# Softmax scaling moved to ScalarE, and weight splits and the filter network moved in the engines' orders, in a two-block fp32 network

## The chip, the cores and the metric

One core of a Trainium2 chip runs the whole program. Five engines work beside each other and meet at semaphores: PE (TensorE) multiplies matrices, DVE (VectorE) and ACT (ScalarE) do elementwise work and read PSUM, POOL (GpSimd) does elementwise work in SBUF, SP (SyncE) issues most DMA transfers. Each engine takes its own instructions in the order in which they are written. The metric is the device time of one execution in microseconds (us).

## The reference

All is fp32, on 256 tokens of 1024 features. A first block gets modulation vectors from `c` (adaLN), mixes tokens by a Hyena convolution and by neighbourhood attention (NA) over 8 heads, and ends in a mixture of experts by product keys (PEER). A second block has two layers of attention, a state-space scan and a gated network. Cut to what the change touches:

```python
def adaln(cond, p):                       # c and c_ctx
    m = jax.nn.silu(cond) @ p['w_ada'] + p['b_ada']
...
def hyena_filters(L, p):
    h = jnp.sin(freq * (feats @ p['hy_f1_w'] + p['hy_f1_b']))
    h = jnp.sin(freq * (h @ p['hy_f2_w'] + p['hy_f2_b']))
    h = jnp.sin(freq * (h @ p['hy_f3_w'] + p['hy_f3_b']))
    h = (h @ p['hy_f4_w']).reshape(L, HY_ORDER, 2, D_HY)
    h = h * jnp.exp(-t * deltas)[:, None, None, :]
    h = h / jnp.sum(jnp.abs(h), axis=(0, 2), keepdims=True)
...
def neighbourhood_attention(q, k, v, k_ctx, v_ctx, rpb):   # per head
    s_loc = jnp.where(col_mask, (q . k) * scale + bias, NEG_INF)
    s_ctx = (q . k_ctx) * scale
    p = jax.nn.softmax(jnp.concatenate([s_loc, s_ctx], axis=-1), axis=-1)
    out = p_loc . v + p_ctx . v_ctx
...
def token_mixer(h, p, attend):
    gate = jax.nn.sigmoid(z[..., COL_G_HY:N_PROJ])
    merged = gate[..., :D_MODEL] * y_hy + gate[..., D_MODEL:] * y_na
    return merged @ p['w_out']
```

## The kernel before

**Weights.** Every weight matrix streams from HBM as chunks of 128 x 1024 fp32 (512 KB) into `wring`, a ring of 6 slots; chunk c goes into slot c modulo 6. SP issues the transfers (L838) in the order of the list that `weight_order(turn)` makes, each as soon as the chunk that is 6 before it in the list has been used. Most matmuls are made of three products of a high and a low part. For such a chunk ACT copies the high part into `w_hi` (`weights_high`, L1440, one op of 128 x 1024), and then the low part `w_lo` is made by POOL (L2809 and L2811, two halves of 128 x 512) or by DVE (L1876). The split ring has 4 places. Activations are split alike: ACT writes `a_hi` from PSUM (`read_high`, L1447), DVE `a_lo` (`read_low`; L1953, L1930). PE multiplies at L877.

**The order.** `psum_order()` lists every PSUM bank use as a pair (name, number); its position in the list is its turn. `weight_order` gives each chunk the turn at which it is done with. In ACT's program, a chunk's split is written where the turn of the bank that ACT is about to read passes the turn at which the slot of that chunk is done with (`due`, called by `wait_filled`), or where `weights_upto(act, name, l, n)` asks for all splits up to chunk n of that name. So the done turn of a chunk is no semaphore: it decides where in ACT's queue a later split stands.

**Opening.** `ada(i)`, i = 0 to 3, multiplies the two condition vectors by four chunks of `w_ada` each (8 matmuls of 2 rows by 512), ACT copies the row out (`ada_row_out`, L1451), PE turns it into columns (`ada_columns`, L965), DVE adds the bias (`ada_out`). Between them runs the filter network: `mlp` 0 to 2 with a Sin by ACT (L1507), and then 8 `filter` matmuls; DVE forms even and odd parts, PE transforms them (`dftf`).

**Neighbourhood attention**, loop over h = 0 to 8, on all engines one step after the other; in step h the turning, the values and `a_hi` belong to head h − 1. For head h DVE adds the bias to the scores in PSUM (L1960), takes the negative maximum (L2259); ACT does exp with the row sum (`read_out`, L1451, `asum`); DVE takes the reciprocal (L2268) and scales the probabilities `nap` (L2270, 128 x 512, in place); PE turns them (`nap`, L945), ACT copies them back (L1451), PE multiplies by the values (`nao`), ACT makes `a_hi` (L1447) and DVE `a_lo` (`na_low`, L1953). Beside this, PE computes the gates of the mixer from `w_in`, two chunks per head from chunk 40 on (`gate`; DVE adds their bias at L2230), and DVE computes the remaining modulation columns as dot products (`ada_dots`, L2241), three chunks of `w_adaT` per head, each in the slot that held no split chunk. The list of chunks per head is w_in, w_in, adaT, adaT, adaT. So chunk 50, the first w_in of head 3, takes the slot of chunk 44, the third adaT of head 1, and so on in steps of five. After head 8 come the products with `w_hy_out` and `w_na_out` (`mix`, read with the gates by DVE at L2294), the late dots, and `w_out`.

**After it** come the norm, the PEER queries (`w_pq`), the gather, and the two layers of the second block. There, the attention's exps of the second half of the tokens (`exponentials(1, 14)`, L1730) stand in ACT's queue with the splits of `w2_z` 14 and 15 between them; `w2_o` is the output projection, whose sums of squares (`norm_tiles`, L1471) ACT takes; `tiles_turned` turns the normed tiles on PE (L957) after DVE's scaling (L1904).

The quoted part that decides on the turn edit is the list of chunks of one head:

```python
for h in range(1, NA_HEADS + 1):
    for k in range(2):
        ...
        w.append(("w_in", None, 12 + 4 * c + kp, CHUNK, done, kp == 3, True))
    w.extend(("w_adaT", None, DOTS_PER_HEAD * (h - 1) + i, CHUNK, turn[("nao", h - 1)] + 1, True, False)
             for i in range(DOTS_PER_HEAD))
```

## Time and profile before

| | us |
|---|---|
| median of 3 runs | 2207.86 |
| lowest, highest | 2206.05, 2212.0 |
| the profiled execution | 2212.09 |
| its span in the profile | 2210.3 |
| PE busy | 1984.0 (90%) |
| DVE busy | 1377.4 (62%) |
| POOL busy | 1048.6 (47%) |
| ACT busy | 1002.8 (45%) |

The times of the rows below are those of the profiled execution, counted from the span's start. An engine's idle time before an operation stands in brackets with what ended it. A wait for several semaphores is put down to the one that came last. The stages lie as follows: opening to 56 us, Hyena to 210, NA to 304, mix and `w_out` to 376, PEER to 1080, the two layers of the second block from there to 1645 and to the end.

### The profile page before, as it was taken

The numbers are of one execution on the slowest core, as the hardware profiler recorded it, in microseconds if no ns is written. First come the engines' busy times: TensorE is split into PE (matmuls) and PEld (weight loads), VectorE is DVE, ScalarE is ACT, GpSimd is POOL, SyncE is SP. The second block draws the span as 40 slices with busy tenths as digits, with TensorE's granted clock in tenths as the row PEclk, the third lists the DMA queues.
The fourth block names the chain that finished last, engine by engine and source line by source line (L and its number), as shares of the span: only waits on it lengthen the run. The fifth ranks groups of instructions, "written<-read, shape, count | busy, mean of one in ns | idle before, by whom it ended". The sixth has DMA issues, their size and how long they took to land.

```text
span 2210.3 us, 27141 instructions
## 1 busy us (share of the span) xinstructions
PE 1984.0 (90%) x9640; PEld 1469.2 (66%) x9640; DVE 1377.4 (62%) x2782; ACT 1002.8 (45%) x1836; POOL 1048.6 (47%) x840
## 2 busy tenths in 40 slices
PE   7999968987877787777999999999999999998998
PEld 1777756943323333333599777889989977777998
DVE  3768955486666676665457754167763775326776
ACT  1623435332222212212445687455564567845555
POOL 2362657764444444443387757900028865692000
PEclk9999979999898989999999999999999999999999
DMA  9242765699999999999655444545555534454553
GB/s 350 68 138 82 253 222 174 211 421 421 422 422 421 421 421 422 421 422 421 229 178 172 136 162 159 173 157 187 187 156 189 181 124 155 160 180 163 191 182 114
DMA packets 111447, 534.40 MB, mean 242 GB/s; under 512 B 12496, under 2 KB 12880, under 8 KB 77904
## 3 DMA queue, kind: packets, MB, share of 16 engines
q1 hardware_dynamic: 67104, 244.72, 33.1%
q0 software_dynamic: 38720, 275.96, 30.4%
q10 hardware_dynamic: 5488, 11.98, 1.7%
q8 instruction: 77, 1.26, 0.2%
q14 instruction: 58, 0.48, 0.1%
HBM read 531.49 MB, written 1.11 MB: 241 GB/s over the span
## 4 chain that ended last, share of the span: by engine, by line
PE 59%; DMA 22%; DVE 6%; ACT 6%; issue 3%; POOL 3%; ACTq 0%; POOLq 0%; DVEq 0%; SPq 0%
PE psum L877 57%; DMA pair_rows<-in_peer_uv,arena 11%; DMA arena<-in_peer_uv,arena 6%; DMA wring<-in_peer_uv,arena 3%; PE psum L945 2%; ACT w_hi L1440 2%; POOL w_lo L2811 2%; POOL w_lo L2809 1%; ACT arena L1451 1%; ACT arena L1785 1%; DVE arena L2551 1%; DMA wring<-in_w_in_hy 1%; DMA wring<-in_w_ada 0%; ACT arena L1730 0%; DVE arena L2567 0%
## 5 line engine op out<-in xcount | busy, mean ns | idle before, releaser
L2809 POOL TENSOR_TENSOR w_lo<-wring,w_hi 128x512 fp32r<-128x512 f32 x280 | 382.4, 1366 | 543.8 <-ACT w_hi L1440 535.5
L1440 ACT ACTIVATE w_hi<-wring 128x1024 fp32r<-128x1024 f32 (+1 forms) x414 | 433.7, 1054 | 334.4 <-PE psum L877 313.0
L877 PE MATMUL psum<-w_hi,a_hi 128*128 128x512 f32 (+1 forms) x1056 | 425.1, 403 | 44.8 <-POOL w_lo L2811 15.2
L877 PE MATMUL psum<-w_lo,a_hi 128*128 128x512 f32 (+1 forms) x1056 | 412.9, 391 | 0.0
L877 PE MATMUL psum<-w_hi,a_lo 128*128 128x512 f32 (+1 forms) x1056 | 412.3, 390 | 0.0
L877 PE MATMUL psum<-arena 128*128 128x512 f32 (+7 forms) x1142 | 336.3, 451 | 65.2 <-ACT arena L1658 50.7
L2811 POOL TENSOR_TENSOR w_lo<-wring,w_hi 128x512 fp32r<-128x512 f32 x280 | 394.8, 1410 | 0.0
L877 PE MATMUL psum<-a_hi,w_hi 128*128 128x256 f32 x1312 | 376.7, 287 | 4.1 <-DVE a_lo L1930 2.3
L877 PE MATMUL psum<-a_hi,w_lo 128*128 128x256 f32 x1312 | 372.0, 284 | 0.0
L877 PE MATMUL psum<-a_lo,w_hi 128*128 128x256 f32 x1312 | 371.9, 283 | 0.0
L877 PEld LDWEIGHTS psum<-arena 128*128 128x128 f32 (+2 forms) x1142 | 186.0, 198 | 198.0 <-issue 126.6
L877 PE MATMUL psum<-pair_rows,arena 128*128 128x512 f32 x512 | 247.2, 631 | 55.3 <-ACT arena L1658 55.3
L877 PEld LDWEIGHTS psum<-w_hi,a_hi 128*128 128x128 f32 x1056 | 201.4, 191 | 99.0 <-POOL w_lo L2811 18.0
L877 PEld LDWEIGHTS psum<-a_hi,w_hi 128*128 128x128 f32 x1312 | 252.2, 192 | 6.8 <-POOL w_lo L2811 3.0
L877 PEld LDWEIGHTS psum<-a_lo,w_hi 128*128 128x128 f32 x1312 | 252.5, 192 | 0.7
L877 PEld LDWEIGHTS psum<-a_hi,w_lo 128*128 128x128 f32 x1312 | 252.3, 192 | 0.0
L877 PEld LDWEIGHTS psum<-pair_rows,arena 128*128 128x128 f32 x512 | 100.4, 201 | 195.9 <-issue 118.0
L877 PEld LDWEIGHTS psum<-w_lo,a_hi 128*128 128x128 f32 x1056 | 201.7, 191 | 42.2 <-issue 3.9
L877 PEld LDWEIGHTS psum<-w_hi,a_lo 128*128 128x128 f32 x1056 | 201.4, 191 | 42.2
L2853 POOL DMA_INDIRECT pair_rows<-in_peer_uv,arena x128 | 137.3, 1072 | 162.8 <-PE psum L877 153.5
L1876 DVE TENSOR_TENSOR w_lo<-wring,w_hi 128x1024 fp32r<-128x1024 f32 x134 | 164.0, 1224 | 62.6 <-ACT w_hi L1440 59.1
L1653 ACT ACTIVATE arena<-arena 128x4 f32<-128x4 f32 (+2 forms) x69 | 14.3, 207 | 333.9 <-DVE arena L2428 333.9
(261 smaller groups left out, 2393.7 us busy)
## 6 DMA issues: line engine op xcount, KB each, us to landing
wring<-in_w_up SPq DMA_DIRECT2D x88, 512.0 KB, 3.3
wring<-in_w_xbc SPq DMA_DIRECT2D x48, 512.0 KB, 3.3
wring<-in_w_dn SPq DMA_DIRECT2D x44, 512.0 KB, 3.3
wring<-in_w_adaT SPq DMA_DIRECT2D x32, 512.0 KB, 4.3
wring<-in_w_qkv SPq DMA_DIRECT2D x32, 512.0 KB, 3.6
wring<-in_w_z SPq DMA_DIRECT2D x32, 512.0 KB, 3.2
wring<-in_w_g SPq DMA_DIRECT2D x32, 512.0 KB, 3.3
wring<-in_w_ps SPq DMA_DIRECT2D x32, 512.0 KB, 3.3
```

Of the source, the lines that this page charges most:

```text
L877: mm = lambda o, a, b, start, stop: nc.tensor.matmul(o, a, b, start=start, stop=stop, skip_group_check=True)
L945: m = nc.tensor.transpose(o[0:s.shape[-1], j * n:(j + 1) * n], s, ident[0:n, 0:n])
L1440: a.reaches(A(w_hi[:, n % SPLIT_RING, 0:width], wring[:, c % RING, 0:width], ACT.Copy), hi_ready, n + 1)
L1451: a.reaches(A(out_, in_, func, **kw), *read_value(name, i))
L1653: a.reaches(A(pact[:, cols_q], pdot[:, cols_q], ACT.Gelu), S("gelu_ready"), q + 1)
L1785: a.done(A(Lm[:, i % 2, (4 * half + j) * P:(4 * half + j + 1) * P], rows[:, j * P:(j + 1) * P], ACT.Relu, bias=acs_s[:, h:h + 1], scale=-1.0))
L1876: v.reaches(T.tensor_tensor(w_lo[:, r, 0:width], wring[:, c % RING, 0:width], w_hi[:, r, 0:width].bitcast(F32), ALU.subtract), *low_done(n))
L2551: ins = T.scalar_tensor_tensor(out=sc, in0=bank(L + "is", b_)[:, at * n_keys:(at + 1) * n_keys], scalar=wi[:, h:h + 1], in1=sc if h else c ...
L2809: nc.gpsimd.tensor_tensor(w_lo[:, r, 0:half], wring[:, c % RING, 0:half], w_hi[:, r, 0:half].bitcast(F32), ALU.subtract)
L2811: nc.gpsimd.tensor_tensor(w_lo[:, r, half:width], wring[:, c % RING, half:width], w_hi[:, r, half:width].bitcast(F32), ALU.subtract).then_ ...
L2853: pool.indirect_dma_start(out=pair(n), out_offset=None, in_=d["peer_uv"], in_offset=bass.IndirectOffsetOnAxis(ap=pidx[:, g, j:j + 1], axis ...
```

## The change

1. In the opening, `mlp` i comes before `ada` i, the 8 filters before `ada` 3, and what belongs to it on ACT and DVE moves alike: the Sin of step i ahead of the copy of row i, the copy of row 3 behind the first two absolute values, the columns of ada i one step later.
2. The done turn of the adaT chunks is one less. That moves the next split of w_in, made of the chunk that takes the slot of the third dot, from behind the exps of a head to ahead of the `a_hi` of the step before.
3. The 16 scalings of the probabilities are done by ACT (Copy with a scale, L1593 of the changed kernel) and no longer by DVE. The reciprocals come ahead of the three dots.
4. `tiles_turned` opens its banks one by one.
5. The splits of `w_out` 7 and `w2_o` 7 are written ahead of the first sum of squares.
6. The split of `w2_z` 15 is written ahead of the exps of the second half; that of `w2_g` 5 behind the Exp of step 1 of the scan.
7. POOL makes the low part of `w_pq` 1 only after the first modulated low part.

ACT in NA, before: loop step 1 from the copies of the turned probabilities of head 0 (L1451, `arena<-psum`), and step 2. `w_hi` at 108 and 109 are the splits of chunks 50 and 51.

```order
105 L1451 ACTIVATE arena<-psum 128x4x128 [waits psum_filled] x2
106 L1447 ACTIVATE a_hi<-psum 64x256 [waits psum_filled]
107 L1451 ACTIVATE arena,small_values<-psum,small_values 128x512 [waits psum_filled,na_max] x2
108 L1440 ACTIVATE w_hi<-wring 128x1024 [waits weights_used,weights_in2,psum_filled]
109 L1440 ACTIVATE w_hi<-wring 128x1024 [waits weights_used,weights_in3]
110 L1451 ACTIVATE arena<-psum 128x4x128 [waits psum_filled] x2
111 L1447 ACTIVATE a_hi<-psum 64x256 [waits psum_filled]
112 L1451 ACTIVATE arena,small_values<-psum,small_values 128x512 [waits psum_filled,na_max] x2
```

The same place after (L1453, L1442 and L1449 are the L1451, L1440 and L1447 of before; L1593 is the scaled copy). 

```order
106 L1442 ACTIVATE w_hi<-wring 128x1024 [waits psum_filled,weights_in4]
107 L1453 ACTIVATE arena<-psum 128x4x128 [waits psum_filled] x2
108 L1442 ACTIVATE w_hi<-wring 128x1024 [waits weights_used,weights_in2]
109 L1449 ACTIVATE a_hi<-psum 64x256 [waits psum_filled]
110 L1453 ACTIVATE arena,small_values<-psum,small_values 128x512 [waits psum_filled,na_max] x2
111 L1593 ACTIVATE arena<-arena,small_values 128x512 [waits na_inverse] x2
112 L1442 ACTIVATE w_hi<-wring 128x1024 [waits weights_used,weights_in3,psum_filled]
113 L1453 ACTIVATE arena<-psum 128x4x128 [waits psum_filled] x2
114 L1442 ACTIVATE w_hi<-wring 128x1024 [waits weights_used,weights_in1]
```

The split with `weights_in2` now stands ahead of `a_hi` and of the exps, and the two scaled copies stand between the exps and the second split.

DVE in NA, before: the three dots of head 1 (L2241; each op of two rows) and what follows.

```order
210 L2241 ISA wring,small_values<-wring,dve_junk 128x1024 [waits weights_in0,c_row_ready]
211 L2241 ISA small_values 128x1
212 L2241 ISA wring,small_values<-wring,dve_junk 128x1024 [waits weights_in1]
213 L2241 ISA small_values 128x1
214 L2241 ISA wring,small_values<-wring,dve_junk 128x1024 [waits weights_in2]
215 L2241 ISA small_values 128x1
216 L2268 RECIPROCAL small_values<-small_values 128x1 [waits bank_read4]
217 L2270 TENSOR_SCALAR arena<-arena,small_values 128x512 [waits vector_steps]
218 L2268 RECIPROCAL small_values<-small_values 128x1 [waits bank_read5]
219 L2270 TENSOR_SCALAR arena<-arena,small_values 128x512 [waits vector_steps]
220 L1953 TENSOR_TENSOR a_lo<-psum,a_hi 64x256 [waits read_high,psum_filled]
221 L1960 TENSOR_TENSOR psum<-psum,arena 128x256 [waits bank_read6,psum_filled]
```

After (L2260 is the dot, L2285 the reciprocal, L1971 the low half, L1978 and L2278 score bias and maximum).

```order
207 L2285 RECIPROCAL small_values<-small_values 128x1 [waits bank_read4]
208 L2285 RECIPROCAL small_values<-small_values 128x1 [waits bank_read5]
209 L2260 ISA wring,small_values<-wring,dve_junk 128x1024 [waits weights_in0,c_row_ready]
210 L2260 ISA small_values 128x1
211 L2260 ISA wring,small_values<-wring,dve_junk 128x1024 [waits weights_in1]
212 L2260 ISA small_values 128x1
213 L2260 ISA wring,small_values<-wring,dve_junk 128x1024 [waits weights_in2]
214 L2260 ISA small_values 128x1
215 L1971 TENSOR_TENSOR a_lo<-psum,a_hi 64x256 [waits read_high,psum_filled]
216 L1978 TENSOR_TENSOR psum<-psum,arena 128x256 [waits bank_read6,psum_filled]
```

The reciprocals moved ahead of the dots and the scalings are gone, so that the low half of the head's output follows the dots directly.

ACT in the second block, before, at the exps of the second half of the tokens (L1730).

```order
595 L1451 ACTIVATE arena<-psum 128x512 [waits psum_filled] x2
596 L1730 ACT_TABLE_LOAD
597 L1730 ACTIVATE arena,small_values<-arena,small_values 128x256 [waits max2]
598 L1730 ACTIVATE arena,small_values<-arena,small_values 128x256 x4
599 L1440 ACTIVATE w_hi<-wring 128x1024 [waits psum_filled,weights_in2]
600 L1730 ACTIVATE arena,small_values<-arena,small_values 128x256 x3
```

After (L1741 is the exp):

```order
603 L1453 ACTIVATE arena<-psum 128x512 [waits psum_filled] x2
604 L1442 ACTIVATE w_hi<-wring 128x1024 [waits psum_filled,weights_in2]
605 L1741 ACT_TABLE_LOAD
606 L1741 ACTIVATE arena,small_values<-arena,small_values 128x256 [waits max2]
607 L1741 ACTIVATE arena,small_values<-arena,small_values 128x256 x7
```

The split with `weights_in2`, of `w2_z` 15, moved from amid the exps to ahead of the first.

```diff
--- before.py
+++ after.py
@@ -267,8 +267,8 @@
     for i in range(3):
-        ada(i), g.append(("mlp", i))
-    ada(3), g.extend(("filter", i) for i in FILTER_ORDER), g.append(("adaT", 3))
+        g.append(("mlp", i)), ada(i)
+    g.extend(("filter", i) for i in FILTER_ORDER), ada(3), g.append(("adaT", 3))
     for o in range(2):
@@ -381,7 +381,7 @@
             w.append(("w_in", None, 12 + 4 * c + kp, CHUNK, done, kp == 3, True))
-        w.extend(("w_adaT", None, DOTS_PER_HEAD * (h - 1) + i, CHUNK, turn[("nao", h - 1)] + 1, True, False)
+        w.extend(("w_adaT", None, DOTS_PER_HEAD * (h - 1) + i, CHUNK, turn[("nao", h - 1)], True, False)
                  for i in range(DOTS_PER_HEAD))
@@ -949,9 +949,11 @@
 
-            o = [open_(name, k) for k in range(KD)]
+            o = []
             for t in range(TT):
                 for k in range(KD):
+                    if not t:
+                        o.append(open_(name, k))
                     if k % 4 == 0:
@@ -982,9 +984,6 @@
         for i in range(3):
-            if i == 1:
-                pe.wait_ge(S("consts_in"), 16)
-            ada(i)
             if i == 0:
@@ -993,13 +992,16 @@
             close(mm(o[0:64, 0:SEQ], HW(f"f{i + 1}")[0:64, :], rhs, True, True))
-        ada(3)
+            if i == 1:
+                pe.wait_ge(S("consts_in"), 16)
+            ada(i)
         pe.wait_ge(S("mlp_h"), 3)
         pe.wait_ge(S("f4_in"), 16)
         for i in FILTER_ORDER:
             o = open_("filter", i)
             t, j = i // 4, i % 4
             close(mm(o, mlp_h[0:64, tile(t)], HW("f4")[0:64, j * 512:(j + 1) * 512], True, True))
+        ada(3)
         ada_columns(3)
@@ -1499,15 +1501,15 @@
         for i in range(3):
-            ada_row_out(i)
+            act.wait_ge(S("mlp_arg"), i + 1)
+            a.reaches(A(mlp_h[0:64, :], mlp_u[0:64, :], ACT.Sin), S("mlp_h"), i + 1)
             if i == 0:
                 act.dma_start(arena[:, A_R + f4_at:A_R + hyw_n], d["hyw"][:, f4_at:hyw_n]).then_inc(S("f4_in"), 16)
                 act.dma_start(hyc[:, feats_n:hyc_n], d["hyc"][:, feats_n:hyc_n]).then_inc(S("hyc_in"), 16)
-            act.wait_ge(S("mlp_arg"), i + 1)
-            a.reaches(A(mlp_h[0:64, :], mlp_u[0:64, :], ACT.Sin), S("mlp_h"), i + 1)
-        ada_row_out(3)
+            ada_row_out(i)
         for o_ in range(2):
             if o_:
+                ada_row_out(3)
                 wait_filled(act, "adaT", 3)
@@ -1585,6 +1587,11 @@
                              accum_out=asum[:, 2 * h + t:2 * h + t + 1])
+                for t in range(TT):
+                    i = 2 * h + t
+                    act.wait_ge(S("na_inverse"), i + 1)
+                    a.reaches(A(nap[h % 2][:, t, :], nap[h % 2][:, t, :], ACT.Copy, scale=ainv[:, i:i + 1]),
+                             S("na_prob"), i + 1)
             if h == 0:
@@ -1604,6 +1611,8 @@
         def first_half(i):
+            if i == 0:
+                weights_upto(act, "w_out", None, 7)
             due(act, "wout", i)
@@ -1723,6 +1732,8 @@
                 n_keys = P * (t + 1)
+                if t:
+                    weights_upto(act, "w2_z", l, first + 1)
                 act.wait_ge(S("max2"), TT * l + t + 1)
@@ -1787,10 +1798,12 @@
                         act.dma_start(rows, decay_rows(l, i + 1, half)).then_inc(S(f"decay_rows_in{half}"), 16)
-                    if i:
+                    if i and (i, half) != (1, 1):
                         ahead = 2 * i + 2 + half
                         weights_upto(act, *(("w2_g", l, ahead) if ahead < 16 else ("w2_pa", l, ahead - 16)))
                 a.reaches(A(Lm[:, i % 2, :], Lm[:, i % 2, :], ACT.Exp, scale=-1.0), S("decay_exp"), 8 * l + i + 1)
+                if i == 1:
+                    weights_upto(act, "w2_g", l, 5)
                 for g_ in range(SSD_G if i == 0 else 0):
@@ -1823,7 +1836,12 @@
 
-            norm_tiles(1 + 2 * l, range(4), lambda i: wait_read(act, L + "wo", i))
+            def half_read(i):
+                if i == 0:
+                    weights_upto(act, "w2_o", l, 7)
+                wait_read(act, L + "wo", i)
+
+            norm_tiles(1 + 2 * l, range(4), half_read)
             scaled_high(L + "fT", KD, f"ffnw{l}")
@@ -1986,8 +2004,8 @@
         for i in range(3):
-            if i:
-                ada_out(i - 1)
+            if i == 2:
+                ada_out(0)
             wait_filled(dve, "mlp", i)
@@ -2000,7 +2018,7 @@
             v.reaches(T.tensor_scalar(u, u, 3.1415925, -3.1415925, ALU.min, ALU.max), S("mlp_arg"), i + 1)
-        ada_out(2)
+        ada_out(1)
         dve.wait_ge(S("hyc_in"), 16)
@@ -2046,6 +2064,7 @@
         filters_in(1)
+        ada_out(2)
         ada_out(3)
@@ -2260,15 +2279,12 @@
                 masked_bias(h + 1)
-            if h:
-                ada_dots(DOTS_PER_HEAD * (h - 1), DOTS_PER_HEAD * h)
             for t in range(TT):
                 i = 2 * h + t
                 wait_read(dve, "nas", i)
-                v.done(T.reciprocal(ainv[:, i:i + 1], asum[:, i:i + 1]))
-                v.settle()
-                v.reaches(T.tensor_scalar(nap[h % 2][:, t, :], nap[h % 2][:, t, :], ainv[:, i:i + 1], None, ALU.mult),
-                         S("na_prob"), i + 1)
+                v.reaches(T.reciprocal(ainv[:, i:i + 1], asum[:, i:i + 1]), S("na_inverse"), i + 1)
+            if h:
+                ada_dots(DOTS_PER_HEAD * (h - 1), DOTS_PER_HEAD * h)
             if h:
@@ -2802,7 +2818,7 @@
             if c == chunk_at[("w_pq", None, 1)]:
-                pool.wait_ge(S("tile_scaled"), 4)
+                pool.wait_ge(S("modulated_lo"), 2 * KD + 1)
             if second_block + 2 <= c < second_block + SPLIT_RING:
```

## Rows read from the trace of the kernel before

**Rows 1.** The page: busy time and shares of the engines.
```profile
PE 1984.0 (90%) x9640; PEld 1469.2 (66%) x9640; DVE 1377.4 (62%) x2782; ACT 1002.8 (45%) x1836; POOL 1048.6 (47%) x840
```

**Rows 2.** What PE waited for in the whole run: us, times, longest.
```profile
PE psum L877 <- ACT arena L1658: 132.3, 55, 8.6
...
PE psum L877 <- POOL w_lo L2811: 15.4, 15, 2.3
...
PE psum L877 <- DVE arena L2230: 7.7, 3, 2.8
```

**Rows 3.** Timeline, all engines, head 7: start, length, engine line op, [idle before <-releaser].
```profile
278.25 2.29 DVE L2241 CUSTOM_DVE_ANT_0 wring<-wring,dve_junk 128x1024 f32<-128x1024 f32 x1
...
280.47 0.15 DVE L2268 RECIPROCAL small_values<-small_values 128x1 f32<-128x1 f32 x1
...
280.58 1.44 SPq L838 DMA_DIRECT2D wring<-in_w_in  x2
...
284.59 0.43 DVE L1953 TENSOR_TENSOR a_lo<-psum,a_hi 64x256 fp32r<-64x256 f32 x1
...
286.85 0.69 DVE L2259 TENSOR_REDUCE small_values<-psum 128x1 f32<-128x512 f32 x1
...
287.46 1.22 DVE L2241 CUSTOM_DVE_ANT_0 wring<-wring,dve_junk 128x1024 f32<-128x1024 f32 x1
...
287.57 0.69 ACT L1451 ACTIVATE arena<-psum,small_values 128x512 f32<-128x512 f32 x1 [0.48 <-DVE small_values L2259]
...
288.25 2.00 ACT L1440 ACTIVATE w_hi<-wring 128x1024 fp32r<-128x1024 f32 x2
```

**Rows 4.** Timeline of DVE in head 1, and of SP behind head 7.
```profile
218.49 1.22 DVE L2241 CUSTOM_DVE_ANT_0 wring<-wring,dve_junk 128x1024 f32<-128x1024 f32 x1
...
221.93 0.15 DVE L2268 RECIPROCAL small_values<-small_values 128x1 f32<-128x1 f32 x1
...
292.09 5.89 SPq L838 DMA_DIRECT2D wring<-in_w_hy_out  x4
```

**Rows 5.** Groups from 200 to 330 us: count, busy us, mean ns, idle before.
```profile
L2270 DVE TENSOR_SCALAR arena<-arena,small_values 128x512 f32<-128x512 f32 x16 | 19.1, 1196 | 0.6
...
L1451 ACT ACTIVATE arena<-psum 128x512 f32<-128x512 f32 x16 | 8.6, 592 | 4.5 <-PE psum L945 4.5
```

**Rows 6.** DMA issues of the whole run: count, KB each, median us to landing.
```profile
wring<-in_w_in SPq DMA_DIRECT2D x28, 512.0 KB, 3.6
```

**Rows 7.** Timeline of PE and ACT at the end of the stage.
```profile
304.17 0.47 PE L877 MATMUL psum<-w_hi,a_hi 128*128 128x512 f32 x1 [2.29 <-POOL w_lo L2811]
...
326.29 0.77 PE L877 MATMUL psum<-w_hi,a_hi 128*128 128x512 f32 x1 [13.03 <-DVE arena L2294]
...
313.29 0.38 ACT L1447 ACTIVATE a_hi<-psum 64x256 fp32r<-64x256 f32 x1 [8.98 <-PE psum L877]
```

**Rows 8.** Timeline of ACT and PE in the opening, and 36 to 44 us: DMA share last but one.
```profile
42.32 1.06 ACT L1440 ACTIVATE w_hi<-wring 128x1024 fp32r<-128x1024 f32 x1 [14.83 <-DMA wring<-in_w_in_hy]
...
56.05 2.90 PE L877 MATMUL psum<-arena 128*128 128x512 f32 x3 [4.33 <-issue]
...
36.00:44.00 8.00, 7.22 (x19) 1.37 (x18) 2.65 (x7) 1.68 (x3) 0.54 (x1) 1.00 1.02 418
```

**Rows 9.** Timeline of DVE and PE at w_pq.
```profile
381.47 1.38 DVE L1930 TENSOR_TENSOR a_lo<-arena,a_hi 128x256 fp32r<-128x256 f32 x1
...
382.99 0.36 PE L877 MATMUL psum<-a_hi,w_hi 128*128 128x256 f32 x1 [2.31 <-DVE a_lo L1930]
```

**Rows 10.** Timeline of ACT and PE at w2_z 15 of the first layer.
```profile
1253.83 0.51 ACT L1730 ACTIVATE arena<-arena,small_values 128x256 f32<-128x256 f32 x1 [6.75 <-DVE small_values L2590]
...
1256.32 1.04 ACT L1440 ACTIVATE w_hi<-wring 128x1024 fp32r<-128x1024 f32 x1
...
1259.99 0.50 PE L877 MATMUL psum<-w_hi,a_hi 128*128 128x512 f32 x1 [2.12 <-POOL w_lo L2811]
```

**Rows 11.** Timeline of PE at w2_o 7 of the first layer.
```profile
1441.64 0.47 PE L877 MATMUL psum<-w_hi,a_hi 128*128 128x512 f32 x1 [1.06 <-POOL w_lo L2811]
```

## The prediction

> **What bounds the kernel now.** I read the page first. PE is busy for nine tenths of the span [rows 1], so time can come back only where PE waits, and the list of PE's waits says where [rows 2]. The longest entry, 132.3 us behind ScalarE's L1658, lies in the PEER gather, in which the change touches nothing. What the change can reach is the 15.4 us of waits for a low half by GpSimd (15 of them, 2.3 at most), the 7.7 us for the gate bias L2230 of VectorE (3 waits [rows 2]) and a single wait of 13.03 us for L2294 [rows 7]. The last two lie in the neighbourhood attention (NA, 210 to 326 us). There the timeline of one head shows VectorE working without a gap: score bias and maxima, three dots, two reciprocals with two scalings, gate bias, low half of the head's output [rows 3]. The first dot of head 1 begins at 218.49 [rows 4] and that of head 7 at 287.46 [rows 3]: 68.97 / 6 = 11.5 us per head. A change of 6.6 us (0.3%) is about what can be told from none.
>
> **Scaling by ScalarE.** It takes 16 TENSOR_SCALAR from VectorE, 19.1 us in all, or 2 x 1.2 per head [rows 5]. ScalarE gets 16 scaled copies; the nearest row is its copy out of PSUM, 0.59 us for the same 128 x 512 [rows 5], so 16 x 0.59 = 9.4 us on an engine that idles more than it works in this stretch (45% busy over the span [rows 1]; an exp of the pair begins at 287.57 [rows 3]). Were VectorE still the bound, a head would cost 11.5 − 2.4 = 9.1, and PE, whose own work per head is about 11.5 − 7.7/6 = 10.2, would bound it. That would be the whole gain, and it is not what I expect, because of the next edit.
>
> **The due turn of the adaT chunks.** By one turn less, ScalarE's split of the next w_in chunk (L1440) stands ahead of the copy a_hi (L1447) that ends a loop step, and so ahead of all that follows on it; the order fences show both. Now follow the slots. The ring has 6, and chunk 50 takes the slot of chunk 44, the third dot's operand; so do 55, 60, … 75 and the first w_hy_out. The SP row proves the dependence: the transfer of w_in is issued at 280.58 [rows 3], 0.1 after the third dot ended at 280.47. Before, that chunk's split came after the exps (288.25), long after it had landed, and a_hi didn't wait for it. After, the things stand in a ring, each waiting for the one before:
> third dot's end, 0.1 to the issue; 3.45 for the transfer (the median over the 28 of w_in is 3.6 [rows 6]; I take a little less, since these go alone); 1.1 for the split (2.00 for two [rows 3]); 0.4 for a_hi [rows 7]; from the start of the low half, L1953, over two score biases to the end of the second maximum, 286.85 + 0.69 − 284.59 = 2.95 [rows 3]; the last exp with its accumulator, 0.8, and a reciprocal, 0.3 with its waits; three dots at 1.15 [rows 4], of which one runs beside GpSimd and takes 2.29 instead [rows 3], so 3.45 + 1.1.
> Sum: 0.1 + 3.45 + 1.1 + 0.4 + 2.95 + 1.1 + 4.55 = 13.6 (13.65) us per head, where it was 11.5. The copies, the turning on PE (3 us per head with its copies out) and the gate bias lie inside the 4.5 us in which the ring waits for the transfer.
> Head 1 is late already: the dots now follow the reciprocals, and these the exps, the Silu with its table loads and the copies; they end at 226.0 by my count, not 221.93 [rows 4]. Six heads later, 226.0 + 6 x 13.6 = 307.6, where they ended at 292.1 [rows 4] (SP issues a slot the moment they end): +15.5. Behind it slack is used up. PE's 2.29 us wait at 304.17 for GpSimd [rows 7] and the like take 3.5 of it, so that a_hi of head 8 comes at 325.3 and not 313.29 [rows 7]; the late dots (one of which waited for its transfer before) take 1.7 more. PE starts mix 2, behind L2294, at 336.6 instead of 326.29 [rows 7]: +10.3. A replay of the queues with the same durations gives +12.7, and −4.4 without the turn edit. **I take +11, range +6 to +14** (a ring of 12.8 to 14.1).
>
> The rows thus make the transfer a quarter of the ring, 3.45 of 13.6. The Trainium skill (DMA: Bandwidth & Descriptors, "Anatomy of one DMA") puts it at some 2.0 us fixed plus bytes over 436 GB/s, so 3.2 here, mostly a part that bandwidth doesn't buy. By it the ring would be 13.4 and the term some 1.5 smaller, 6 x 0.25; it speaks against putting a transfer into a chain, since that part can't be bought off.
>
> **The opening.** The filter network goes ahead of the modulation rows and the filters ahead of the last row. This stretch is fed by DMA: its share is 1.02 from 36 to 44 [rows 8], and ScalarE sits 14.83 us until the first w_in_hy chunk lands at 42.3 [rows 8], whatever PE did before. The copy of the ada 2 row still stands behind that split, so filters 6 and 7, which need its bank, still start near 44. Then ada 3, some 7 us of matmuls, comes after them and not before, and its row copy stands behind two more splits; against this, the even and odd sums on VectorE begin earlier, beside less of GpSimd. PE's dftf begins at 56.05 after 4.33 idle [rows 8]; I get 54.7 to 56.6. **0, −2 to +2.**
>
> **w_pq.** Low parts on GpSimd that ran beside the modulation's low part (L1930, 1.38 us [rows 9], where an operation of the same 256 columns takes 0.43 [rows 3]) wait for it. PE's wait of 2.31 [rows 9] loses 1.38 − 0.43, or 1.0. **−1**, at worst 0: GpSimd's own part then comes later by about as much.
>
> **w2_z 15, twice.** The split stands amid the exps of the second half, at 1256.32 [rows 10], and PE waits 2.12 us for the low half made from it [rows 10]. Moved ahead of these exps it comes 2.5 us or more earlier, in a time when ScalarE idles (6.75 us before 1253.83), and covers that. The exps also end 1.0 earlier. What it costs: GpSimd now runs beside VectorE's small dt chain, by my estimate +1.5, which the 1.0 and the cover above 2.12 take up. **−2.0 per layer, −4 in all**, range −7 to 0.
>
> **w_out 7 and w2_o 7.** Split ahead of the norm's squares. In each layer PE waits 1.06 us [rows 11] at this place: −1.06 x 2 = **−2**, range −2 to 0. In the first block GpSimd is busy without a gap ahead of that chunk, and an earlier split helps nothing. The moved split of w2_g 5 and the banks of the turned tiles opened one by one cost and bring nothing: PE waits there for VectorE's L1904, which is not touched, and the banks are long read.
>
> **Sum:** 0 + 11 − 1 − 4 − 2 = +4. Against the profiled execution (2212.09, of which the span is 2210.3) that is 2216; that execution lies 4.2 above the median of 2207.86, from which I forecast **2212**.
>
> **Rivals.**
> *No ring* (faster). The splits don't hold ScalarE: the transfers are early, or PE is the bound anyway. For it: all of VectorE's 2.4 us per head do go. Then the three waits of 7.7 and the one of 2.3 go, and the late chain is up to 4 shorter: NA −10 to −14, total 2207.9 − 12 − 7 = about 2190. Against it: the order, and the issue 0.1 after the dot. Chance 0.15.
> *A longer ring* (slower than before). The second split of each head now follows the exps and the scaled copies, so that GpSimd's low halves come onto the dots. One dot beside them is in my sum; if it is two, each head costs 1.1 more: 14.7, and 6 x 1.1 = 6.6 on top: 2218.6. It decides as soon as the second split starts under 2 us after the first dot. With it, or with the upper end of the ring (+14) at the main forecast, the time is over 2214.5. Chance 0.16.
> *No dot collides* (the ring stands, but is shorter). A dot takes 2.29 beside GpSimd [rows 3] and 1.15 alone [rows 4]. With the scalings gone GpSimd may be through before any dot: 12.5 per head, term 11 − 6.6 = +4.4, total 2205. The Trainium skill (GPSIMD Engine Reference, "Specifications") has GpSimd share its SBUF interface with VectorE instructions in a two-port mode or with two SBUF inputs; the dots are of the second kind, so by it the collision stays as long as the two overlap, and it gives no reason for them not to. Chance 0.07.
>
> **Chances.** The forecast, ring of about 13.6: 0.62, of it 0.47 within 0.3% (2201.2 to 2214.5) and 0.15 above. Faster: 0.15. Same: 0.47 + 0.07 = 0.54. Slower: 0.15 + 0.16 = 0.31. For 8 in 10 the range goes from 2198 (the edge of the first rival; its middle is left out) to 2220, which takes in the longer ring.
>
> **What would show it.** In the trace after: first dots of successive heads 13.6 us apart, not 11.5; ahead of a_hi, ScalarE's L1440 idle for 3 to 4 us behind the transfer of w_in, in each head from 2 on; no PE wait for the gate bias, but waits for ScalarE's copies of the turned probabilities; PE's wait behind L2294 again near 13, ending at 336 or so; dftf at 55 to 57; no wait of 2.1 at w2_z 15 and of 1.06 at w2_o 7, while VectorE's dt chain is slower; 1.3 at w_pq where it was 2.31. I am wrong if the heads stand 11.5 or less apart: then the ring isn't there and the time is near 2190. If they stand 13.6 apart and the total doesn't move, the slack behind head 8 was larger than 5 us.

## The result, and the profile after

The changed kernel takes 2243.32 us (median of 4 runs, 2241.44 to 2247.69) where the kernel before took 2207.63: a ratio of 1.0161, with a 95% interval of 1.0140 to 1.0182. It is 35.7 us slower, and outside the range of the prediction (2198 to 2220), whose value was 2212.

The profiled execution has a span of 2242.6 us, 32.3 more than before. The same events in the two traces show where:

| event | before | after | difference | forecast |
|---|---|---|---|---|
| PE starts dftf | 56.05 | 59.99 | +3.9 | −2 to +2 |
| DVE, first reciprocal of the attention | 213.84 | 217.91 | +4.1 | 0 |
| DVE, dots of step 1 begin | 218.49 | 225.32 | +6.8 | +4.1 (their end) |
| DVE, dots of step 7 begin | 287.46 | 328.29 | +40.8 | +15.5 (their end) |
| DVE reads mix 0 (L2294, now L2310) | 324.90 | 360.89 | +36.0 | +10.3 |
| first gather of PEER | 416.70 | 451.56 | +34.9 | +10 |
| layer 1, first load of the decay rows | 1274.45 | 1309.56 | +35.1 | +8 |
| layer 2, first load of the decay rows | 1837.01 | 1871.12 | +34.1 | +5 |
| last store issued | 2205.82 | 2238.10 | +32.3 | +4 |

So 34 us are lost between the first dots of step 1 and those of step 7, where 11 were forecast: one place. PE's waits of the whole run (us in total, times, longest) say what it is waiting for, to be read beside [rows 2]:

```profile
PE psum L877 <- ACT arena L1453: 24.2, 17, 3.6
...
PE psum L877 <- DVE arena L2310: 10.7, 1, 10.7
...
PE psum L877 <- POOL w_lo L2827: 9.9, 13, 1.7
...
PE psum L877 <- DMA arena<-in_hyc: 9.4, 1, 9.4
...
PE psum L945 <- DVE a_lo L1971: 8.0, 3, 4.8
...
PE psum L877 <- DVE a_lo L1971: 7.7, 6, 2.0
...
PE psum L877 <- DVE arena L2249: 7.1, 2, 4.4
```

The gate bias (L2249, the L2230 of before) still costs 7.1, there is a new group of 8.0 for `a_lo` L1971, and ScalarE's copies L1453 come to 24.2. With the due turn undone (e1 below) the first two are gone and the third is 15.9: these are links of one chain. The other two lines are not: 9.4 is PE's start in the opening, and the 7.7 for `a_lo` is 7.8 in e1 too. The timeline of the changed kernel over one turn of it, from the end of the dots of step 4 to the dots of step 5, with the lines of four engines put in order of time (start, length, engine line op, [idle before <-releaser]):

```profile
282.52 1.47 SPq L838 DMA_DIRECT2D wring<-in_w_adaT  x2
...
284.81 0.80 SPq L838 DMA_DIRECT2D wring<-in_w_in  x2
...
289.73 1.06 ACT L1442 ACTIVATE w_hi<-wring 128x1024 fp32r<-128x1024 f32 x1 [10.19 <-DMA wring<-in_w_in]
...
290.81 0.38 ACT L1449 ACTIVATE a_hi<-psum 64x256 fp32r<-64x256 f32 x1
...
291.30 0.43 DVE L1971 TENSOR_TENSOR a_lo<-psum,a_hi 64x256 fp32r<-64x256 f32 x1 [5.31 <-ACT a_hi L1449]
...
293.56 0.69 DVE L2278 TENSOR_REDUCE small_values<-psum 128x1 f32<-128x512 f32 x1
...
294.55 0.55 POOL L2839 DMA_DIRECT2D arena<-in_rpb  x1 [13.16 <-DVE small_values L2278]
...
295.12 1.29 POOL L2825 TENSOR_TENSOR w_lo<-wring,w_hi 128x512 fp32r<-128x512 f32 x1
...
295.22 5.94 DVE L2260 CUSTOM_DVE_ANT_0 wring<-wring,dve_junk 128x1024 f32<-128x1024 f32 x1
...
298.80 1.26 POOL L2827 TENSOR_TENSOR w_lo<-wring,w_hi 128x512 fp32r<-128x512 f32 x1
...
301.09 0.08 DVE L2260 DVE_READ_ACCUMULATOR2_ANT small_values<- 128x1 f32 x1
```

The third dot of the step ends at 284.70. SP issues w_in at 284.81. ScalarE sits 10.19 us, until it has landed at 289.73, in front of a split, and its `a_hi` follows at 290.81. VectorE then takes the low half, biases and maxima, to 294.25. GpSimd, whose queue holds the rpb transfer until that maximum, gets through to its low halves only now, at 295.12, and makes four of them in one piece, to 300.06. The first dot of VectorE, which is on record from 295.22, is done at 301.1, 1.1 us after GpSimd's last half: 5.94 us where it took 1.22 [rows 3]. The ring closes at 303.38, 18.7 us after 284.70. From step 1 to step 7 the first dots start 13.5, 19.5, 18.2, 18.7, 18.7 and 14.4 apart, 103.0 in all. Forecast were 6 x 13.6 = 81.6, and before it was 69.0.

PE pays twice. Between 250 and 280 us before, and 260 and 290 after, the columns are: stretch, its length, busy us (count) of PE, PEld, DVE, ACT and POOL, PE's granted clock, DMA share, GB/s.

```profile
250.00:280.00 30.00, 27.54 (x132) 22.12 (x130) 28.94 (x44) 14.15 (x26) 18.20 (x12) 1.00 0.68 229
```

```profile
260.00:290.00 30.00, 20.65 (x65) 15.45 (x66) 19.44 (x22) 7.62 (x15) 8.65 (x8) 0.70 0.48 167
```

With a third of the time idle, PE is granted 0.70 of full speed, that is the lower of its two levels (1.2 GHz) for six tenths of the stretch, where it had the upper one (2.4 GHz) throughout.

### The profile page after: what moved, and what is told of

Same layout as the page of the kernel before. It is cut to its first block, busy times and chain, and to the rows that moved or that the text cites. A ratio compares the mean times of both kernels' runs of the same rounds, so it can differ in the third digit from the quotient of the medians.

```text
span 2242.6 us, 27134 instructions
## 1 busy us (share of the span) xinstructions
PE 1996.3 (89%) x9640; PEld 1477.1 (66%) x9640; DVE 1378.4 (61%) x2766; ACT 1011.7 (45%) x1852; POOL 1032.1 (46%) x840
## 3 DMA queue, kind: packets, MB, share of 16 engines
q8 instruction: 77, 1.26, 0.2%
## 4 chain that ended last, share of the span: by engine, by line
PE 56%; DMA 24%; DVE 8%; ACT 6%; issue 4%; POOL 2%; another core or an unknown queue 0%; ACTq 0%; DVEq 0%; POOLq 0%; SPq 0%
PE psum L877 54%; DMA pair_rows<-in_peer_uv,arena 10%; DMA arena<-in_peer_uv,arena 8%; DMA wring<-in_peer_uv,arena 3%; DVE wring L2260 2%; ACT w_hi L1442 1%; PE psum L945 1%; DMA wring<-in_w_in 1%; ACT arena L1453 1%; POOL w_lo L2827 1%; POOL w_lo L2825 1%; DMA wring<-in_w_in_hy 1%; DVE arena L2567 1%; DVE arena L2583 0%; DVE small_values L2278 0%
## 5 line engine op out<-in xcount | busy, mean ns | idle before, releaser
L2825 POOL TENSOR_TENSOR w_lo<-wring,w_hi 128x512 fp32r<-128x512 f32 x280 | 374.4, 1337 | 551.6 <-ACT w_hi L1442 541.3
L1442 ACT ACTIVATE w_hi<-wring 128x1024 fp32r<-128x1024 f32 (+1 forms) x414 | 434.7, 1054 | 399.6 <-PE psum L877 310.3
L877 PE MATMUL psum<-w_hi,a_hi 128*128 128x512 f32 (+1 forms) x1056 | 425.2, 403 | 36.8 <-DVE arena L2310 10.7
L877 PE MATMUL psum<-arena 128*128 128x512 f32 (+7 forms) x1142 | 343.4, 458 | 85.3 <-ACT arena L1667 49.5
L2827 POOL TENSOR_TENSOR w_lo<-wring,w_hi 128x512 fp32r<-128x512 f32 x280 | 388.4, 1387 | 0.0
L877 PE MATMUL psum<-pair_rows,arena 128*128 128x512 f32 x512 | 254.1, 647 | 65.9 <-ACT arena L1667 65.9
L877 PEld LDWEIGHTS psum<-w_hi,a_hi 128*128 128x128 f32 x1056 | 202.0, 191 | 90.6 <-POOL w_lo L2827 13.4
L2869 POOL DMA_INDIRECT pair_rows<-in_peer_uv,arena x128 | 142.2, 1111 | 177.2 <-PE psum L877 166.8
L1662 ACT ACTIVATE arena<-arena 128x4 f32<-128x4 f32 (+2 forms) x69 | 14.3, 207 | 335.7 <-DVE arena L2444 335.7
```

Source lines behind the costliest of these rows:

```text
L877: mm = lambda o, a, b, start, stop: nc.tensor.matmul(o, a, b, start=start, stop=stop, skip_group_check=True)
L1442: a.reaches(A(w_hi[:, n % SPLIT_RING, 0:width], wring[:, c % RING, 0:width], ACT.Copy), hi_ready, n + 1)
L1662: a.reaches(A(pact[:, cols_q], pdot[:, cols_q], ACT.Gelu), S("gelu_ready"), q + 1)
L2825: nc.gpsimd.tensor_tensor(w_lo[:, r, 0:half], wring[:, c % RING, 0:half], w_hi[:, r, 0:half].bitcast(F32), ALU.subtract)
L2827: nc.gpsimd.tensor_tensor(w_lo[:, r, half:width], wring[:, c % RING, half:width], w_hi[:, r, half:width].bitcast(F32), ALU.subtract).then_ ...
L2869: pool.indirect_dma_start(out=pair(n), out_offset=None, in_=d["peer_uv"], in_offset=bass.IndirectOffsetOnAxis(ap=pidx[:, g, j:j + 1], axis ...
```

## The experiments

All are compared with the kernel before on the same chip. In the four comparisons that kernel took 2207.63, 2209.44, 2211.20 and 2212.39 us, so kernels of different comparisons are better set against each other by their ratios than by their times. "A" below is the changed kernel, "B" the one before.

**e1: the due turn undone in A.**

```diff
-        w.extend(("w_adaT", ..., CHUNK, turn[("nao", h - 1)], True, False)
+        w.extend(("w_adaT", ..., CHUNK, turn[("nao", h - 1)] + 1, True, False)
```

> The changed kernel with one edit undone: the done turn of the adaT chunks is again turn + 1, so that the split of the next w_in chunk stands behind the exps. Theory (ring: third dot, transfer of w_in, split, a_hi, maxima, exps, dots): the loop steps of the attention go from 18.7 us back to 11.5 or less, the first dots no longer last 5.9 us, and the 31.9 us lost in the attention (36.0 at L2310 less 4.1 ahead of it) go: 2243.3 - 31.9 = 2211 or, if the gates that VectorE no longer delays come too, down to 2201. Rival (the scaled copies on ScalarE hold up its queue and are the loss): the steps stay above 15 us and the time above 2230.

Measured: 2203.66 against 2209.44, ratio 0.9972 (0.9961 to 0.9983). One number of the table takes the kernel from 1.6% slower to 0.3% faster. DVE's dots in it:

```profile
256.16 1.23 DVE L2260 CUSTOM_DVE_ANT_0 wring<-wring,dve_junk 128x1024 f32<-128x1024 f32 x1
...
258.46 0.08 DVE L2260 DVE_READ_ACCUMULATOR2_ANT small_values<- 128x1 f32 x1
...
266.65 1.23 DVE L2260 CUSTOM_DVE_ANT_0 wring<-wring,dve_junk 128x1024 f32<-128x1024 f32 x1
```

The steps start 11.3 and 11.1 and from then on 10.5 us apart (before: 11.5 in the mean), no wait of PE for the gate bias is left, and no first dot is long. The third still takes 2.29 beside GpSimd. The scaled copies are not the loss.

**e2: the due turn alone, in B.**

```diff
-        w.extend(("w_adaT", ..., CHUNK, turn[("nao", h - 1)] + 1, True, False)
+        w.extend(("w_adaT", ..., CHUNK, turn[("nao", h - 1)], True, False)
```

> The kernel before with one edit alone: the done turn of the adaT chunks one less. Theory (ring): it is closed here too, without the exps and the reciprocal in it, since the dots stand ahead of the reciprocals: 13.6 - 1.1 = 12.5 us per step if dots take 1.15 and one 2.3, and up to 16 if GpSimd's four low halves come in one piece onto a dot. 6 steps of 1 to 4.5 us more: 2214 to 2235. Rival (scaled copies are the loss): about 2208.

Measured: 2239.47 against 2209.44, ratio 1.0129 (1.0105 to 1.0153), above the upper end of what I expected (2214 to 2235). The first dots start 14.8, 18.9, 18.2, 18.4, 18.2 and 13.2 us apart, where I had at most 16: the long dot takes 6.4, and w_in is issued 4.1 to 6.3 us before its split begins. The ring closes without any scaled copy in it. One turn, ACT, POOL and DVE:

```profile
285.20 1.06 ACT L1440 ACTIVATE w_hi<-wring 128x1024 fp32r<-128x1024 f32 x1 [11.14 <-DMA wring<-in_w_in]
...
290.02 0.55 POOL L2823 DMA_DIRECT2D arena<-in_rpb  x1 [12.89 <-DVE small_values L2259]
...
290.24 6.41 DVE L2241 CUSTOM_DVE_ANT_0 wring<-wring,dve_junk 128x1024 f32<-128x1024 f32 x1
...
294.26 1.29 POOL L2811 TENSOR_TENSOR w_lo<-wring,w_hi 128x512 fp32r<-128x512 f32 x1
```

The split waits 11.14 us for the transfer; the rpb transfer lets GpSimd through at 290.02, and the dot is on record for 6.41 us, until 1.1 us after GpSimd's last half.

**e4: the low halves ahead of the rpb transfer, in A.**

```diff
             if h >= 2:
+                if h >= 4:
+                    weights_upto(pool, "w_in", None, 12 + 2 * (h - 2))
                 due(pool, "nas", 2 * (h - 2) + 1)
```

> The changed kernel, with GpSimd told to make the low part of the first w_in chunk of a step ahead of its rpb transfer, which waits for the maximum of that step. Theory (the dot of 5.9 us waits for four low halves in one piece, because the rpb transfer holds back two of them in GpSimd's queue): the first dots of steps 2 to 5 fall from 5.9 to 1.2 or 2.3 us, the steps from 18.7 to 14 or 15, and the time by 4 x 3.6 to 4 x 4.7 = 14 to 19 us to 2225 - 2229. Rival (the dot is slow because of the DMA transfers in flight or a port shared with ScalarE): dots stay near 5.9 and the time near 2243.

Measured: 2226.65 against 2209.44, ratio 1.0078 (1.0053 to 1.0103); that is 16.7 us less than A by the medians and 18 by the ratios, whose intervals leave 11 to 26. POOL and DVE:

```profile
276.64 1.29 POOL L2825 TENSOR_TENSOR w_lo<-wring,w_hi 128x512 fp32r<-128x512 f32 x1 [4.30 <-ACT w_hi L1442]
...
280.33 0.56 POOL L2841 DMA_DIRECT2D arena<-in_rpb  x1 [1.15 <-DVE small_values L2278]
...
280.99 1.22 DVE L2260 CUSTOM_DVE_ANT_0 wring<-wring,dve_junk 128x1024 f32<-128x1024 f32 x1
...
283.11 1.38 POOL L2825 TENSOR_TENSOR w_lo<-wring,w_hi 128x512 fp32r<-128x512 f32 x1 [2.23 <-ACT w_hi L1442]
...
283.29 0.08 DVE L2260 DVE_READ_ACCUMULATOR2_ANT small_values<- 128x1 f32 x1
...
294.46 1.23 DVE L2260 CUSTOM_DVE_ANT_0 wring<-wring,dve_junk 128x1024 f32<-128x1024 f32 x1
```

GpSimd makes two low halves at 276.64, while the ring is elsewhere, the first dot takes 1.22, and only the third meets the other two halves. The steps are (309.79 − 223.85) / 6 = 14.3 us in the mean, single ones 13.4 to 15.7. Nothing else was changed, so the long first dot is GpSimd's piece of four. Between the first dots of steps 1 and 7 this trace is 17.0 us shorter than A's: 4 x 3.6 = 14.4 of it are the dots, 2.5 the transfers of w_in. The mean of 14.3 is the ring as forecast (13.6) with 0.7 more. The transfer accounts for that: from issue to split it takes 3.75, 5.56, 3.47, 4.25, 3.51 and 5.23, in the mean 4.3 where 3.45 was reckoned.

**e6: scaling on ScalarE alone, in B** (reciprocals ahead of the dots, 16 scaled copies on ACT, nothing else; the edit is that of the diff above).

> The kernel before with one part alone: scaling of the probabilities by ScalarE, reciprocals ahead of the dots; the done turn stays. Theory: 2.4 us per step leave VectorE, the three waits of PE for the gate bias (7.7 us) go and the step is PE's 10.2 us or somewhat more: 2207.6 - 5 to - 10 = 2198 to 2203. Rival (the chain exps, reciprocals, dots is longer than what left, since VectorE now waits for ScalarE ahead of the dots): steps stay at 11.5 and the time within 3 us of 2207.6.

Measured: 2206.49 against 2209.44, ratio 0.9985 (0.9971 to 0.9998). The first dots of steps 6 and 7 stand at 275.83 and 286.32, 10.5 apart. The steps are the theory's; the time is nearly the rival's. It gives 3 us, less than the 5 to 10 expected, since the dots of step 1 begin 7.4 us after the first reciprocal of the attention (215.66 and 223.07) and not 4.65 (213.84 and 218.49): the reciprocals ahead of them wait 2.13 for exps that stand behind the Silu and its table loads.

**e3: the opening edit alone, in B** (all of `psum_order`, PE, ACT and DVE ahead of the spectra as in the diff).

> The kernel before with the opening edit alone. Theory (filters 6 and 7 wait for the bank of ada 2, whose copy stands on ScalarE behind the split of w_in_hy 0; ada 3 and the four ring slots of its chunks come late, so that the later w_in_hy chunks are issued 15 us later than before): dftf starts at 60 instead of 56.05 and the time is 2209.4 + 3.9 = 2213. Rival (the stages behind have slack and take it up): dftf at 60, time within 1.5 us of 2209.4.

Measured: 2210.33 against 2211.20, ratio 1.0004 (0.9991 to 1.0017). PE's two waits in the opening, and the stretch behind it:

```profile
44.88 3.78 PE L877 MATMUL psum<-arena 64*128 64x512 f32 x4 [3.54 <-ACT arena L1451]
...
59.37 0.41 PE L965 MATMUL psum<-consts,arena 2*128 2x2 f32 x4 [2.01 <-ACT arena L1451]
...
57.00:100.00 43.00, 40.35 (x231) 28.44 (x231) 27.77 (x62) 26.85 (x46) 13.15 (x11) 1.00 0.28 100
```

The same stretch of the kernel before:

```profile
57.00:100.00 43.00, 42.36 (x240) 30.06 (x239) 30.37 (x68) 25.91 (x44) 10.65 (x9) 0.97 0.14 43
```

dftf starts at 59.7 and is late by 2 to 4 us (55.75 to 57.64 in the seven kernels with the old opening), as the theory says: filters 6 and 7 wait 3.54 for the bank of ada 2, and ada 3 comes late. But the time doesn't follow. From 57 to 100 us PE is granted 1.00 here and 0.92 to 0.97 in the kernels with the old opening, and the first reciprocal of the attention comes at 215.9, where those seven have 213.8 to 216.7. A granted clock that is higher by 0.03 to 0.08 over 43 us, in which PE is busy nearly throughout, is worth 1.3 to 3.4 us of its work, by my estimate. The rival was right: what is behind takes it up. (e1 and e4, with the same opening, have 1.00 too, and 216.0 and 216.4. The profile of A has 0.96 and 217.9: 0.04 over 43 us is 1.7 us, about what it is later than the others. Why the clock fell there and not in the others stays open.)

**e8: half of the opening edit, in B** (mlp ahead of ada, ada 3 still ahead of the filters).

> The kernel before with half of the opening edit: mlp i ahead of ada i, but ada 3 still ahead of the filters. Theory (the loss is the place of the filters, the 3.1 us later start of PE is made good because the weights bound this stretch): PE starts at 9.3, dftf at 54.5 to 56.5, time 2207.5 to 2210. Rival (the loss is the late start): dftf near 59, time near 2213.

Measured: 2213.51 against 2211.20, ratio 1.0017 (1.0009 to 1.0026).

```profile
44.62 0.41 PE L965 MATMUL psum<-consts,arena 2*128 2x2 f32 x4 [2.02 <-ACT arena L1451]
...
44.96 12.87 PE L877 MATMUL psum<-arena 64*128 64x512 f32 x16
...
57.00:100.00 43.00, 42.37 (x219) 28.28 (x219) 28.71 (x65) 24.68 (x42) 7.57 (x7) 0.93 0.09 27
```

My theory of the opening falls with this run: the half that I held for harmless costs 3.8 us by the ratio (2 to 6 by its interval), with dftf at 58.28 and the clock at 0.93 behind it. The numbers are those of the rival. But the late start isn't the whole path to them: behind the wait of 2.02 for ScalarE's copy the filter matmuls take 12.87 us, mostly at the lower clock (0.58 granted from 44 to 57), where they take 7.14 in the kernel before. The old opening shows both cases too: in e2, e5, e7 and e10 PE waits 1.8 to 2.1 us there, the clock is 0.50 from 44 to 57, and dftf starts at 57.1 to 57.6; in the kernel before, e6 and e9 it waits 0.8 or less, the clock is 0.83 to 0.92, and dftf starts at 55.8 to 57.2. Whether the other half, the place of the filters, takes the 3.8 us back is not shown: the intervals of e3 and e8 overlap. Why PE waits for the copy in one kernel and not in another with the same opening stays open.

**e5: w2_z 15 and w2_o 7 alone, in B.**

```diff
                 n_keys = P * (t + 1)
+                if t:
+                    weights_upto(act, "w2_z", l, first + 1)
                 act.wait_ge(S("max2"), TT * l + t + 1)
...
+            def half_read(i):
+                if i == 0:
+                    weights_upto(act, "w2_o", l, 7)
+                wait_read(act, L + "wo", i)
```

> The kernel before with two edits alone: w2_z 15 split ahead of the second exps, w2_o 7 ahead of the squares. Theory: in the two layers the traces of before and of the changed kernel differ by 37.1 - 32.3 = 4.8 us at their ends, all of it from these two: 2209.4 - 4.8 = 2204.6, PE's waits of 2.1 and 1.06 gone. Rival (part of the 4.8 is noise of the two profiles, which moved 2 us against each other in the gather): -3 or less, 2206.4.

Measured: 2208.98 against 2211.20, ratio 0.9996 (0.9987 to 1.0004). Not 4.8 us, and not clear of nothing. POOL, DVE and PE where the split of w2_z 15 now stands:

```profile
1247.87 1.26 POOL L2816 TENSOR_TENSOR w_lo<-wring,w_hi 128x512 fp32r<-128x512 f32 x1 [0.26 <-ACT w_hi L1440]
...
1247.99 1.22 DVE L1974 SCALAR_TENSOR_TENSOR dve_junk<-dve_junk,small_values 128x64 f32<-128x64 f32 x1
...
1249.25 1.16 DVE L1971 TENSOR_SCALAR dve_junk<-dve_junk 128x64 f32<-128x64 f32 x1
...
1250.44 0.22 DVE L1974 SCALAR_TENSOR_TENSOR small_values<-small_values,dve_junk 128x64 f32<-128x64 f32 x1
...
1251.67 0.83 PE L877 MATMUL psum<-small_values,consts 128*128 128x32 f32 x6 [2.00 <-DVE a_lo L1960]
```

The wait of 2.1 for the low half is gone, and one of 2.00 for VectorE's `a_lo` stands in its place: the operations of the dt chain ahead of it have 64 columns and take 1.2 us beside GpSimd's low half, 0.22 behind it. From the issue of w_small to the first load of decay rows a layer takes 164.7 to 165.2 us with the edit, in 10 layers of 5 kernels. Without it, it takes 165.7 in 7 layers and 164.1 in 5 of six kernels; in the mean 165.0 without and 164.9 with it. In the longer ones PE runs at a lower clock behind its wait of 2.1, as in the kernel before (clock 0.66 in the stretch 1260 to 1265):

```profile
1260.00:1265.00 5.00, 5.00 (x18) 4.02 (x19) 2.08 (x1) 4.33 (x7) 4.65 (x3) 0.66 0.37 113
```

**e7: the parts that I held for good, together**: scaling, w2_z 15, w2_o 7 and w_pq in B; opening, due turn and the rest as before.

> The changed kernel without its two bad parts: scaling on ScalarE, w2_z 15, w2_o 7 and the w_pq wait, but the opening and the done turn of before. Theory (parts add up): scaling -3, late splits -4.8, w_pq -0.8: 2209.4 - 8.6 = 2200.8, and 2.9 below the kernel with the opening edit (2203.66). Rival (the parts share slack, so that the sum is less): 2204.

Measured: 2203.15 against 2211.20, ratio 0.9972 (0.9963 to 0.9981). This is the ratio of e1 (0.9972), which has four more of the edits: the opening, w_out 7, w2_g 5 and the banks opened one by one. None of the last three was run alone. The parts don't add up to the 8.6 us of the theory; 0.28% is 6.2 us, nearer to the rival.

**e10: the same without w2_z 15.**

> Scaling on ScalarE, w2_o 7 and the w_pq wait, but the split of w2_z 15 amid the exps as before: the kernel e7_scaling_late_pq less one edit. Theory (the removed wait of 2.1 us came back as a wait of 2.0 us for VectorE's a_lo, since GpSimd's low halves then run beside the dt chain; from the issue of w_small to the first decay load a layer takes 164.7 us with the edit and 165.7 or 164.1 without): 0.9 us per layer or less, 2203 to 2205. Rival (the edit is worth its 2.1 per layer): 2207.5.

Measured: 2201.86 against 2212.39, ratio 0.9952 (0.9937 to 0.9967). I expected up to 1.8 us more than e7; it is 1.3 less by the medians and 4 by the ratios, whose intervals just overlap. Nothing speaks for the edit of e5. PE's wait is there:

```profile
1255.66 0.50 PE L877 MATMUL psum<-w_hi,a_hi 128*128 128x512 f32 x1 [2.09 <-POOL w_lo L2818]
```

But the clock stays at 1.00 behind it in this profile, and both layers take 164.06.

**e9: the same with w2_z 15 split behind the first exp of the second half.**

```diff
                     if h in (2, 5):
                         weights_upto(act, "w2_z", l, first + (h == 5))
+                    if t and h == 1:
+                        weights_upto(act, "w2_z", l, first + 1)
```

> The same kernel, with the split of w2_z 15 behind the first exp of the second half instead of behind the fifth or ahead of all. Theory: the low halves begin some 2 us earlier than before, so that PE's wait of 2.1 us falls to under 0.3, and they no longer meet the dt chain, so that no wait of 2.0 us for a_lo comes: from w_small to the first decay load 163.6 to 164.1 us, and 1 us per layer below e10: 2201 to 2203. Rival (the chain of exps that now carries the split within it ends 1.0 later and is late itself): as e10.

Measured: 2199.19 against 2212.39, ratio 0.9937 (0.9921 to 0.9953). The two marks of the first layer:

```profile
1102.85 0.33 SPq L838 DMA_DIRECT2D wring<-in_w_small  x1
...
1266.82 0.34 ACTq L1781 DMA_DIRECT2D dve_junk<-acs_rows  x1
```

They are 163.97 us apart, 163.94 in the second layer, and neither the wait for the low half nor that for `a_lo` is left. This is the fastest kernel of the study, 0.6% faster than the one before. It is clear of e7 (intervals up to 0.9953 and from 0.9963), but not of e10: the medians are 2.7 us apart, and the intervals overlap. Nor do the two profiles show a gain: a layer is 0.1 us shorter than in e10, where the clock didn't fall; against a layer in which it does, at 165.7, it is 1.7 shorter.

## Why the prediction was wrong, point by point

**The ring was right, its price was not.** The prediction named the due turn as what decides, drew the ring with its links, and gave it +11 (+6 to +14). The runs show 1.29%, 28.5 us, for it alone (e2), and 1.61 + 0.28 = 1.89%, 42 us (39.7 by the medians), between A and A without it (e1). The ring sets the mean step to 16.9 and 17.2 us in the two cases, and takes it from 11.5 in the one and 10.7 in the other, which is some 5 us of the difference; the rest isn't accounted for. In the sum of the ring two terms were mis-sized, the first of them because a wait in GpSimd's queue was overlooked. The six turns take 103.0 us where 81.6 were forecast. The dots make up 4 x 3.6 = 14.4 of the 21.4 us, and the transfers, 28.3 us where 6 x 3.45 = 20.7 were reckoned, the rest.

*"three dots ..., of which one runs beside GpSimd and takes 2.29 instead"*: three dots take 8.2 us in steps 2 to 5, not 4.55. I took over from [rows 3] how a dot and GpSimd meet before, and followed every queue around the moved split but GpSimd's. There the low halves of that split stand behind the rpb transfer, which waits for this step's maximum. Before, the split came behind the exps anyway and the transfer was never in its way; moved ahead, its low halves are held until the dots begin. In the turns from step 1 to 2 and from 6 to 7, whose dots meet no such piece, the forecast holds: 13.5 and 14.4. With the halves let through (e4) it is 14.3 in the mean. The term was short by 14.4 us in the trace, and the run without the long dot is 16.7 us faster.

*"3.45 for the transfer ..., since these go alone"*: they don't. Two adaT chunks are issued from 282.52 on, as their dots end 1.15 apart, and w_in behind them. From issue to split w_in takes 3.56, 5.76, 4.64, 4.92, 5.06 and 4.31 us in the six turns. It is tempting to blame the short distance of the requests, but in e4, where the third dot is 2.28 and the requests lie further apart in every turn, it still took 5.56 and 5.23 in two turns of six. What makes it long stays open. The 3.2 us that the prediction works out from the Trainium skill (DMA: Bandwidth & Descriptors, "Anatomy of one DMA") are too low as well; the page fits its figure to transfers that GpSimd issues, and these are SP's.

**Step 1** was forecast to end its dots at 226.0; it ends at 229.9, and 226.0 plus the 4.1 that the attention begins late is 230.1. **Behind step 7** I had 5.2 us of slack; it was 40.8 − 36.0 = 4.8. PE's wait behind mix is there again, 10.7 after 13.03. ScalarE's wait for the transfer, forecast at 3 to 4 us in each head, was 5.2 and 5.9 in the turns with short dots and 9.9 to 11.0 in the others, since ScalarE comes to the split early and the long dot delays the issue.

**Scaling on ScalarE.** The prediction has VectorE at 9.1 a head and PE, at about 10.2, as the bound; the steps are 10.5 in e1 and e6. "No PE wait for the gate bias" was wrong for A (7.1 us, in turns with a long dot) and right for e1. The rival "no ring" was priced at 2190, where e1 takes 2204, since the prediction took all waits as gains and let no later start of step 1 count against them.

**The opening, 0, −2 to +2.** Of the start of dftf that was wrong in this trace (+3.9), of the time it was right (e3), for a reason that I hadn't given. I said that filters 6 and 7 start near 44 as before; they do, at 44.78, but PE idles 3.57 ahead of them and ada 3 is still to come. "I get 54.7 to 56.6" left out that ada 3's matmuls then run in part at the lower clock: they take 9.41 us and not some 7 (granted clock 0.64 from 44 to 57), and a wait of 1.41 follows.

**w2_z 15, −2.0 per layer.** Wrong. The step that failed: "GpSimd now runs beside VectorE's small dt chain, by my estimate +1.5, which the 1.0 and the cover above 2.12 take up". The 1.5 is on PE's path, as a wait of 2.0. Net it is −0.4 (e5, by the ratio) or nothing (e10). **w2_o 7** went as forecast at its place, the wait of 1.06 is gone in both layers; at **w_pq** the wait of 2.31 is 0.62, where 1.3 was forecast. In the time of the run their 2 and 1 us can't be told from scatter.

**What I took for proof.** The sum of traces gave −4.8 for the late edits; a run of them alone gave −0.9 by the ratio (−2.2 by the medians). One profile of each kernel differs by 1 to 3 us in stretches where nothing was changed.

The chance of "slower" was 0.31, and the rival "a longer ring" pointed to the right cause, GpSimd's halves on the dots, with a price of 6.6 on top; it counted one more dot of 2.29 and not one dot behind a whole piece.

## What to carry to other kernels

When a split, a load or any other wait is moved up in one engine's queue, follow what it releases into the queue of every engine that takes part, and ask what stands ahead of it there: here the largest part of the price was in GpSimd's queue, which the prediction hadn't followed. Before moving anything by one place, look whether its transfer is released by work that itself waits for what stands behind it; a ring through a transfer costs its whole latency in each turn, here 3.6 to 5.8 us, six times. A wait that is removed by moving work to where it meets other work can come back, as here one of 2.1 as one of 2.0: look for the place where the work meets nobody (behind the first exp), not for the earliest.

## What the hardware showed that I hadn't expected

A VectorE dot over two SBUF operands, which takes 1.22 us alone, was on record for 5.94 and 6.41 us while GpSimd made four low halves of 1.26 us back to back, and GpSimd's weren't lengthened. Before, the same two met with the dots first (277 to 282 us): GpSimd's halves took 2.17 and 2.25 instead of 1.27, the first two dots 1.22 and the third 2.29. The Trainium skill (GPSIMD Engine Reference, "Specifications") says that the two engines share an SBUF interface and that instructions with two SBUF inputs contend there; the traces agree. In the second case neither waited for more than one operation of the other; in the first the dot waited until all four halves had ended. In e2 the dot's record begins 0.35 us before the first half's, so that being first on record doesn't decide it; what does is open.

The clock's share in the time was larger than I reckoned with: a layer at 165.7 or at 164.1 us with the same program, by whether PE ran some 3.4 us at the lower level behind a wait of 2.1; and an opening whose late end of 2 to 4 us was made good, for 1.3 to 3.4 us by the same estimate, by 1.00 instead of 0.92 to 0.97 in the 43 us behind it.
